# The rows of maxima and floors of the matrix heads: spread over the partitions by DMA copies instead of full-float products

## The reference, cut to what matters

```python
i_pre, f_pre = gates[..., :ML_HEADS], gates[..., ML_HEADS:]
...
m_t = jnp.maximum(inter, jnp.max(dmat, axis=-1))
w_intra = jnp.exp(dmat - m_t[..., None])
...
sw = w_intra * jnp.einsum('bhcld,bhcsd->bhcls', qc, kc)
...
den = jnp.maximum(jnp.abs(den_raw), jnp.exp(-m_t))
hc = num / den[..., None]
```

## Time and profile before

| | us |
|---|---|
| median of three runs | 2802.95 (2801.0 to 2803.54) |
| the profiled execution's own time | 2793.8 |
| its span | 2791.6 |
| TensorE busy | 2741.2 (98%) |
| VectorE busy | 1532.4 (55%) |
| ScalarE busy | 1110.5 (40%) |

### The profile page before, as it was taken

The page is one execution under the profiler, slowest core; times in us unless marked ns, Lnnn a source line. Parts: engine busy times, 40 slices in busy tenths (PEclk is TensorE's granted clock), DMA queues, the critical chain, the costliest instruction groups (busy, mean ns, idle before and its releaser), DMA issues.

```text
span 2791.6 us, 33679 instructions
## 1 busy us (share of the span) xinstructions
PE 2741.2 (98%) x12745; PEld 2240.1 (80%) x12745; DVE 1532.4 (55%) x2107; ACT 1110.5 (40%) x1521; POOL 42.8 (2%) x36
## 2 busy tenths in 40 slices
PE   9999999999999999999999999999999999999998
PEld 7887788887888778888878878888878668788886
DVE  4376755455535675554667654434563556644344
ACT  3146544334313654432352443322442654533223
POOL 3000000000200000000000000000000000000000
PEclk9999999999999999999999999999999999999999
DMA  5221233332332123333243423333242114232322
GB/s 161 90 61 54 83 93 99 94 100 83 104 97 72 50 69 106 90 94 102 79 121 91 121 76 91 94 102 100 80 106 72 36 48 134 61 105 83 108 84 87
DMA packets 463902, 249.89 MB, mean 90 GB/s; under 512 B 21094, under 2 KB 459327, under 8 KB 463679
## 3 DMA queue, kind: packets, MB, share of 16 engines
q1 hardware_dynamic: 463807, 248.57, 31.1%
HBM read 246.44 MB, written 2.10 MB: 89 GB/s over the span
## 4 chain that ended last, share of the span: by engine, by line
PE 89%; DVE 6%; ACT 3%; issue 1%; DMA 1%; DVEq 0%; ACTq 0%; SPq 0%
PE M L711 26%; PE M L713 26%; PE M L712 26%; DVE w_lo L2134 1%; PE M L804 1%; PE M L806 1%; PE M L805 1%; PE A L901 1%; PE A L876 1%; PE A L711 1%; PE A L945 1%; PE A L712 1%; PE A L713 1%; PE A L890 0%; ACT w_hi L1514 0%
## 5 line engine op out<-in xcount | busy, mean ns | idle before, releaser
L711 PE MATMUL M<-h_hi,w_hi 128*128 128x512 f32 x2184 | 860.8, 394 | 1.0 <-issue 1.0
L713 PE MATMUL M<-h_hi,w_lo 128*128 128x512 f32 x2184 | 851.6, 390 | 0.0
L712 PE MATMUL M<-h_lo,w_hi 128*128 128x512 f32 x2184 | 851.4, 390 | 0.0
L1514 ACT ACTIVATE w_hi<-stage 128x1024 fp32r<-128x1024 f32 (+3 forms) x504 | 495.6, 1026 | 725.5 <-PE M L713 661.0
L2134 DVE TENSOR_TENSOR w_lo<-stage,w_hi 128x1024 fp32r<-128x1024 f32 (+3 forms) x504 | 584.7, 1198 | 148.4 <-ACT w_hi L1514 147.7
L711 PEld LDWEIGHTS M<-h_hi,w_hi 128*128 128x128 f32 x2184 | 410.6, 188 | 92.1 <-issue 5.7
L713 PEld LDWEIGHTS M<-h_hi,w_lo 128*128 128x128 f32 x2184 | 410.5, 188 | 86.6
L712 PEld LDWEIGHTS M<-h_lo,w_hi 128*128 128x128 f32 x2184 | 410.7, 188 | 86.2 <-issue 2.6
L711 PE MATMUL M<-hid_hi,w_hi 128*128 128x512 f32 x704 | 275.2, 391 | 7.0 <-DVE hid_lo L2272 7.0
L713 PE MATMUL M<-hid_hi,w_lo 128*128 128x512 f32 x704 | 274.0, 389 | 0.0
L712 PE MATMUL M<-hid_lo,w_hi 128*128 128x512 f32 x704 | 274.0, 389 | 0.0
(11 more groups left out here) (491 smaller groups left out, 3230.6 us busy)
## 6 DMA issues: line engine op xcount, KB each, us to landing
stage<-in_w_up SPq DMA_DIRECT2D x88, 512.0 KB, 4.5
stage<-in_ffn_w_gate_up SPq DMA_DIRECT2D x88, 512.0 KB, 4.7
stage<-in_w_in SPq DMA_DIRECT2D x80, 512.0 KB, 4.5
stage<-in_w_down SPq DMA_DIRECT2D x32, 384.0 KB, 3.7
stage<-in_ffn_w_down SPq DMA_DIRECT2D x32, 384.0 KB, 3.8
stage<-in_od_w_in SPq DMA_DIRECT2D x21, 512.0 KB, 4.0
stage<-in_w_down SPq DMA_DIRECT2D x32, 320.0 KB, 3.5
stage<-in_ffn_w_down SPq DMA_DIRECT2D x32, 320.0 KB, 3.5
```

What stands on the lines that cost most here:

```text
L711: pe.matmul(bank, a_hi, b_hi, start=(n == 0), stop=False)
L712: pe.matmul(bank, a_hi, b_lo, start=False, stop=False)
L713: last = pe.matmul(bank, a_lo, b_hi, start=False, stop=(n == k - 1))
L1514: act.activation(w_hi[:, s, part * HALF:part * HALF + n], stage[:, part, 0:n], ACT.Copy)\
```

## The change

The eight full-float products and their waits go. In their place SP issues eight DMA copies, each of one row of 512 numbers on one partition to all 128 partitions. Three of them (maxima 0 and 1, floors 0) stand in SP's list behind the load of chunk 4 of the input projection; the other five (maxima 2, floors 1 to 3, maxima 3) behind the pieces of the third chunk of `od_uq`. The targets are rows in SBUF that are free by then: three of `latent`, and five of the normalised input `h_hi` and `h_lo`, for which SP first waits until TensorE has used chunk 7. The readers take their row from these instead of `A[3]`. The diagonal of heads 0 and 1 waits for the first two copies of maxima, that of heads 2 and 3 for all four; the floors of head 0 wait for one copy, those of the others for all four. `ml_square_sum` gets a wait of its own for the bank.

```diff
+        spare = [h_hi[:, 4 + n, :].bitcast(F32) for n in range(4)] + [h_lo[:, 4, :].bitcast(F32)]
+        ml_tops = (latent[:, 0, :], latent[:, 1, :], spare[0], spare[1])
+        ml_floors = (latent[:, 2, :], spare[2], spare[3], spare[4])
...
+            def spread_row(dst, row, landed_):
+
+                sp.dma_start(dst, row.unsqueeze(1).broadcast_to([1, P, S])).then_inc(landed_, 16)
+
             for n in range(4):
                 load_tiles(c0 + n, tiles, 2 * n)
             for n in range(2):
                 load_wide(c0 + 4 + n, w[:, 0:4 * S], 4 + n)
+                if n == 0:
+                    sp.wait_ge(rows_done, 1)
+                    for h in range(2):
+                        spread_row(ml_tops[h], g_top[h:h + 1, :], ml_top_landed)
+                    sp.wait_ge(floor_set, 1)
+                    spread_row(ml_floors[0], g_sum[0:1, :], ml_floor_landed)
...
+            sp.wait_ge(w_used, start["od_in"][0] + 7 + 3)
+            spread_row(ml_tops[2], g_top[2:3, :], ml_top_landed)
+            for h in range(1, ML_HEADS):
+                spread_row(ml_floors[h], g_sum[h:h + 1, :], ml_floor_landed)
+            spread_row(ml_tops[3], g_top[3:4, :], ml_top_landed)
...
-            def ml_top(h):
-
-                pe.matmul(A[3][:, :], row_of[h], g_top[0:ML_HEADS, :], start=True, stop=True).then_inc(ml_top_done, 1)
-
-            def ml_floor(h):
-
-                pe.matmul(A[3][:, :], row_of[h], g_sum[0:ML_HEADS, :], start=True, stop=True).then_inc(ml_floor_done, 1)
...
                 pe.wait_ge(ml_sq, h + 1)
+                if h:
+                    pe.wait_ge(ml_ln, h)
                 pe.matmul(A[3][:, :], ones, ml_3[:, :], start=True, stop=True).then_inc(ml_ss, 1)
...
-            ml_top(0)
             latent_tiles(c0 + 6, h_hi, h_lo, KT)
...
             ml_score(0)
-            pe.wait_ge(ml_w_done, 1)
-            ml_top(1)
             latent_tiles(c0 + 7, h_hi, h_lo, KT)
...
             ml_values(0)
-            pe.wait_ge(ml_w_done, 2)
-            pe.wait_ge(floor_set, 1)
-            ml_floor(0)
             pe.wait_ge(ml_num_out, 1)
             ml_score(1)
...
-                        act.activation(w[:, ST[st] + P:ST[st] + ST_N[st]], A[3][:, (st + 1) * P:], ACT.Exp,
+                        act.activation(w[:, ST[st] + P:ST[st] + ST_N[st]], ml_tops[h][:, (st + 1) * P:], ACT.Exp,
                                        bias=a_st, scale=-1.0)
...
-                dve.wait_ge(ml_top_done, h + 1)
+                dve.wait_ge(ml_top_landed, 16 * (2 if h < 2 else ML_HEADS))
...
-                                         A[3][:, :].rearrange("p (t c) -> p t c", t=TT), -1.0,
+                                         ml_tops[h].rearrange("p (t c) -> p t c", t=TT), -1.0,
...
-                dve.wait_ge(ml_floor_done, h + 1)
-                dve.tensor_tensor(ml_1[:, :], ml_1[:, :], A[3][:, :], ALU.max).then_inc(ml_den, 1)
+                dve.wait_ge(ml_floor_landed, 16 * (ML_HEADS if h else 1))
+                dve.tensor_tensor(ml_1[:, :], ml_1[:, :], ml_floors[h], ALU.max).then_inc(ml_den, 1)
```

More of the change, by code:

```diff
@@ L375, in block_program @@
         (ml_scores, ml_diag_done, ml_w_done, ml_sw_done, ml_nd, ml_abs, ml_hm, ml_sq, ml_ss, ml_ln, ml_rs, ml_y,
-         ml_hi, ml_out, ml_den, ml_inv, ml_top_done, ml_floor_done, ml_d, ml_num_out) = (
+         ml_hi, ml_out, ml_den, ml_inv, ml_top_landed, ml_floor_landed, ml_d, ml_num_out) = (
             sem("ml_scores"), sem("ml_diag_done"), sem("ml_w_done"), sem("ml_sw_done"), sem("ml_nd"),
             sem("ml_abs"), sem("ml_hm"), sem("ml_sq"), sem("ml_ss"), sem("ml_ln"), sem("ml_rs"), sem("ml_y"),
-            sem("ml_hi"), sem("ml_out"), sem("ml_den"), sem("ml_inv"), sem("ml_top_done"), sem("ml_floor_done"),
+            sem("ml_hi"), sem("ml_out"), sem("ml_den"), sem("ml_inv"), sem("ml_top_landed"), sem("ml_floor_landed"),
             sem("ml_d"), sem("ml_num_out"))
@@ L1253, in latent_tiles @@
                 two_tiles(c, c % 2, operand(hi, lo), k, widths=widths)
-            row_of = [ident[0:ML_HEADS, h:h + 1].broadcast_to([ML_HEADS, P]) for h in range(ML_HEADS)]
             key_banks = [(A[0], 0), (A[1], 0), (A[2], 0), (A[2], 2 * P)]
-            def ml_top(h):
-                pe.matmul(A[3][:, :], row_of[h], g_top[0:ML_HEADS, :], start=True, stop=True).then_inc(ml_top_done, 1)
-            def ml_floor(h):
-                pe.matmul(A[3][:, :], row_of[h], g_sum[0:ML_HEADS, :], start=True, stop=True).then_inc(ml_floor_done, 1)
             def ml_score(h):
@@ L1340, in _ @@
             latent_tiles(q0, cq_hi, cq_lo, 3)
-            pe.wait_ge(ml_den, 1)
-            ml_top(2)
             ml_values(1)
-            pe.wait_ge(ml_w_done, 3)
             ml_square_sum(0)
             latent_tiles(q0 + 1, cq_hi, cq_lo, 3)
-            pe.wait_ge(ml_ln, 1)
-            ml_floor(1)
             pe.wait_ge(ml_num_out, 2)
@@ L1356, in _ @@
             latent_tiles(q0 + 2, cq_hi, cq_lo, 3)
-            pe.wait_ge(ml_den, 2)
-            ml_top(3)
             ml_values(2)
-            pe.wait_ge(ml_w_done, 4)
             ml_square_sum(1)
@@ L1363, in _ @@
             ml_score(3)
-            pe.wait_ge(ml_ln, 2)
-            ml_floor(2)
             latent_tiles(k0, ckv_hi, ckv_lo, 2)
             ml_values(3)
-            pe.wait_ge(ml_den, 3)
-            ml_floor(3)
             latent_tiles(k0 + 1, ckv_hi, ckv_lo, 2)
-            pe.wait_ge(ml_den, 4)
             ml_square_sum(2)
@@ L1447, in _ @@
             scores(1)
-            pe.wait_ge(ml_ln, 3)
             ml_square_sum(3)
```

## The result

The changed kernel takes 2848.16 us, the median of 5 runs (2843.8 to 2850.86), against 2802.95 (5 runs, 2799.11 to 2803.54): ratio 1.0165, 95% interval 1.0151 to 1.0179. That is 45 us between the medians and 46 by the ratio. The forecast was 2850.5.

The account below looks back on a forecast made before the run. TensorE, busy 98% of the span, was taken as the bound up to the rotation, then VectorE and ScalarE. Terms -4.7 + 10.2 + 38.5 + 3.6 = +47.6 us gave 2850.5 us; likeliest case 2844 to 2865, 8-in-10 range 2797 to 2866.

Parts of the forecast that it names:

- The gain of the removed products: Odd mixer, TensorE: of eight removed products only those on the chain of waits count, 4.7 us gained, at most 8.6.
- The time of a copy: SP's queue: spreading one SBUF row to 128 partitions, 256 KB, takes t = 9.6 us, limited by its single source partition.
- the positions' row: One HBM row spread to 128 partitions, 3.9 us to landing; model for the middling rival, t between 2 and 6, chance 0.12.
- the wide read: Output store reading all 128 partitions: lower bound of 0.6 us per copy; copies under 1.9 us are the hidden rival, chance 0.30.
- two forms that I left open: During the stalls: all sixteen engines queue at one source, DMA share near 1, or one engine does it all, near 0.06.
- Group one: Maxima 0 and 1, floors 0, behind chunk 4's load: chunk 5 lands late; free up to t = 6.2 us, costs 10.2.
- Group two: Maxima 2, floors 1 to 3, maxima 3: head 2's diagonal waits for all five; free to t = 1.9, costs 38.5 us.
- break-even: Middling rival, group one free and group two costing 5(t - 1.9): gain and cost balance at t = 2.8; chance 0.12.
- The clock: TensorE behind the two stalls: eight products each time at the 1.2 GHz level, 1.8 us per stall, 3.6 us together.

Follow-up runs that it names:

- copy-free kernel: Changed kernel without the eight copies and their waits, readers taking the existing full tile `rstd`: 2791.1 us against 2796.62 for the kernel before, ratio 0.9984.
- wide source: Changed kernel with the same eight copies and waits, but read from all 128 partitions of `rstd`: ratio 0.9975 to the kernel before.
- half rows: Changed kernel with each copy moving only 256 columns, the others filled with a constant on GpSimd: ratio 1.0035 to the kernel before.
- run at 98 GB/s: Changed kernel with each copy reading partitions 0, 4, 8 and 12 of `rstd`, 32 times each: ratio 0.9997 to the kernel before.
- own semaphores: Changed kernel with the last five copies in the order they are read, each with its own semaphore: ratio 1.0139 to the kernel before.
- group one alone: Changed kernel copying only maxima 0 and 1 and floors 0, the other rows made by the products of before: ratio 1.0028 to the kernel before.

## Why the prediction was right

**The gain of the removed products, 4.7 us: right in kind, low in size.** It is 5.4 us. Up to head 1 1.30 stood for 1.25, up to head 2 2.85 for 2.6. Most of what is missing, 0.4 us, is in the last part, maxima 2 and floors 1, for which I took 2.1; the copy-free kernel gains 2.5 there. The chains show where: the eight products that follow each of these two took 2.35 us before (at 2179.59 and 2190.15) and 2.16 without them, 0.19 us each. I had counted such an effect for the first removed product only. The product of maxima 3 (2199.32) is taken out ahead of the diagonal of head 3, and nothing of it shows there, as forecast; floors 2 and 3 lie behind that diagonal, where no distance here measures them.

**The time of a copy, t = 9.6 us: right.** SP's fourth and fifth issues of group two take 9.73 and 9.81 us, and the rate during the stall is 25 to 30 GB/s. Taking one source partition for a sixteenth of the store's best rate was the right choice out of 0.6 to 11.4, and both faster values fell: the positions' row, whose 3.9 us belong to a source in HBM, and the wide read. Of the two forms that I left open, it is the one with all engines held (share 0.91), and it fits that a second queue brought nothing. The Trainium skill, "SBUF — State Buffer", section "Door 1: The DMA port swizzle", had the figure: 27.2 GB/s for one port, by which a copy is an estimated 9.6 us. The trace agrees, with 26.7 GB/s. The Trainium skill's rule in "DMA: Bandwidth & Descriptors", section "Anatomy of one DMA", 2.0 us plus bytes over 436 GB/s (there a fit to DMAs that GpSimd issues), does not hold for such a copy: the measured one takes 9.8 us, and only the wide source (landings of 3.0 to 6.2 us) comes near to it.

**Group one, 3(t - 6.2) = 10.2 us: right, 10.0.** And free at t = 4.9, as the half rows show. With the measured t = 9.8 the term gives 10.8, so the free part is rather 6.5 us than 6.2, and the two small errors cancel. The route of the cost is the one named: the load of chunk 5 lands behind three copies, its rounding is late.

**Group two, 5(t - 1.9) = 38.5 us: right as a number, incomplete as a cause.** With t = 9.8 the term gives 39.5; VectorE was held 40.5. The run at 98 GB/s, t = 2.7, held it 5.8 us where the term gives 4.0, and came out even; the break-even was forecast at 2.8. The half rows gave 16.4 for 15. So the free part is rather 1.5 to 1.7 us than 1.9. What I did not see is that the key chunks' weights behind the copies are due almost as soon as the rows: the run with own semaphores took away the wait that I had named and still lost 38.8 us, 33 of it to group two. The term should have been put down to the five copies in front of everything that follows on the queue, not to the diagonal's wait alone.

**The clock, 3.6 us: right in kind, and half of it was paid back by something that I left out.** Behind the first stall 2.7 us are lost to products at the lower clock instead of 1.8, for there are 27 of them and not eight. (With the same group one the kernel of group one alone has 25 and that with own semaphores 14, which accounts for most of the difference between their 12.5 and 11.2 us at head 0.) Behind the second stall the clock costs 2.3 us where I took 1.8: the scores of head 2 stand in the chain of waits, and the rotation starts 4.43 us behind them, where it starts 2.16 behind them in the kernel without copies. Yet from the diagonal of head 2 to that of head 3 the kernel after needs 16.99 us, the one without copies 17.35. What pays for the clock is that TensorE did its other products while VectorE was held: the scores start 4.2 us behind the diagonal instead of 7.0. The kernel after, then the one without copies (its diagonal is at 2180.18):

```profile
2245.83 4.64 PE L1278 MATMUL A<-q_m,k_m 128*128 128x512 f32 x8 [37.67 <-ACT ml_2b L1959]
2250.26 2.00 PE L1354 MATMUL M<-q_h,const 128*128 128x512 f32 x4
```

```profile
2187.14 2.32 PE L1267 MATMUL A<-q_m,k_m 128*128 128x512 f32 x8
2189.30 1.88 PE L1343 MATMUL M<-q_h,const 128*128 128x512 f32 x4
```

The sum of the forecast was +47.6 us, and +47.8 is measured at head 3: 12.9 for group one with its clock, 40.6 at head 2, 0.4 regained, less 5.4 of gain. That the sum hits so closely is partly luck: a gain too small by 0.7 and a clock term too large by about 1 pull one way, and 2 us too little for group two the other. One sum of the forecast doesn't come out: with t = 9.0 its terms give 2845.8, and its range began at 2844, which changes nothing here.

## What to carry to other kernels

Before a row is spread by DMA, ask which partitions the reads come from: one partition gave 27 GB/s to all sixteen engines together, and four partitions gave 24, 49 or 98 according to which four. Send the row through HBM once if a round trip of 4 us is covered; that beat the products here (0.9979). Four source partitions 4 apart only came out even with them (0.9997), and no run spreads one row from four partitions that all hold it. And price a slow copy by all that stands behind it, on its own queue and on the shared engines: a wait split off took 7 of group two's 40 us away and moved the rest, and another queue took nothing away.

## What the runs showed of the hardware

- The first two issues of such copies on SP's queue take 0.5 to 0.7 us each, the third 7.0 to 7.4, the fourth and fifth as long as a whole copy (9.7 to 9.8 us with one source partition, 4.9 with half rows). From the wide source each issue took 0.6. From GpSimd's queue each took 0.5 to 0.6, but then SP's issues of weights were held, 17.1 and 21.8 us for two each.
- One row read 128 times from one SBUF partition takes 9.8 us for 256 KB with a DMA share of 0.9; the same from HBM lands in 3.5 to 5.4 us.
- A copy written as 4 partitions times 32 repeats had a DMA share of 0.25, one written as 1 times 128 of 0.91. With partitions 0 to 3 it is even slower than with one (24 against 27 GB/s, a hold of 45.3 us against 40.5), though fewer engines are taken.
- A 512 KB load that ran beside three one-partition copies from another queue landed after 27.6 us instead of 4.1.
